# Forming the first output tile of the first projection during its norm, and moving four modulation pieces to the pooling stage

## The reference, cut to what matters

```
mod_k = silu(c) @ mod_w[k] + mod_b[k]        # k = 0, 1, 2; for c and c_ctx; 1024 x 3072 weights each
h     = layer_norm(x) * (1 + scale) + shift  # shift, scale: the first two thirds of mod_0
p     = h @ w_in                             # 2304 rows x 1024, by 1024 x 4224: 33 tiles of 128 output columns
pool  = (windowed means of p[:, :256] - p[:, :256]) @ pool_w * pool_scale
```

## Time and profile before

| what | us |
|---|---|
| median of 3 runs | 6125.97 (6121.39 to 6126.76) |
| profiled execution, its own time | 6124.45 |
| its span | 6122.5 |
| norm block | about 61 to 251 |
| projection block | about 251 to 1099 |
| pooling block | about 1099 to 1161 |

### The profile page before, as it was taken

One profiled execution on the slowest core, in us unless ns is written; L12 is line 12 of the kernel. 1 busy time (PEld: TensorE's weight loads), 2 busy tenths in 40 slices (PEclk: granted clock), 3 DMA queues, 4 the chain that ended last, 5 costly groups with the idle time before them and its releaser, 6 DMA issues. The chain is left out here.

```text
span 6122.5 us, 127440 instructions
## 1 busy us (share of the span) xinstructions
PE 5220.1 (85%) x55385; PEld 3996.1 (65%) x55385; DVE 3363.5 (55%) x5004; ACT 1889.2 (31%) x2998; POOL 1754.5 (29%) x1381
## 2 busy tenths in 40 slices
PE   6799999599997566587999659999897999688989
PEld 1488888488886455476888435555476888445667
DVE  2226656444444666476895268888755000307877
ACT  1224444233333443134111214444413000015652
POOL 2201111245443555035000006666635111000012
PEclk8899999799998888798999779999998999888999
DMA  6424434211121110373322320000074211221035
GB/s 201 139 97 154 153 139 156 84 60 61 55 64 69 41 52 29 131 230 123 109 105 81 125 87 22 17 16 20 30 220 136 71 67 71 78 69 75 31 108 160
DMA packets 430043, 572.37 MB, mean 93 GB/s; under 512 B 66470, under 2 KB 318246, under 8 KB 416766
## 3 DMA queue, kind: packets, MB, share of 16 engines
q1 hardware_dynamic: 364886, 391.37, 20.3%
q10 hardware_dynamic: 49272, 115.65, 4.9%
q0 software_dynamic: 15344, 57.45, 2.4%
HBM read 361.26 MB, written 203.12 MB: 92 GB/s over the span
## 5 line engine op out<-in xcount | busy, mean ns | idle before, releaser
L157 PE MATMUL p_bank<-p_hT_high,p_w_high 128*128 128x512 f32 (+1 forms) x2784 | 1053.7, 378 | 20.9 <-DVE p_w_low L151 17.0
L158 PE MATMUL p_bank<-p_hT_low,p_w_high 128*128 128x512 f32 (+1 forms) x2784 | 1045.4, 376 | 0.0
L159 PE MATMUL p_bank<-p_hT_high,p_w_low 128*128 128x512 f32 (+1 forms) x2784 | 1045.2, 375 | 0.0
L157 PEld LDWEIGHTS p_bank<-p_hT_high,p_w_high 128*128 128x128 f32 x2784 | 525.4, 189 | 123.9 <-DVE p_w_low L151 17.3
L159 PEld LDWEIGHTS p_bank<-p_hT_high,p_w_low 128*128 128x128 f32 x2784 | 525.7, 189 | 95.5
L158 PEld LDWEIGHTS p_bank<-p_hT_low,p_w_high 128*128 128x128 f32 x2784 | 525.8, 189 | 93.3
L2796 POOL TENSOR_TENSOR at_acc<-at_acc,at_p 128x512 f32<-128x512 f32 x256 | 423.6, 1655 | 143.7 <-ACT at_p L2734 122.5
L2734 ACT ACTIVATE at_p<-at_sc 128x1024 f32<-128x1024 f32 (+1 forms) x296 | 284.8, 1012 | 401.1 <-PE at_sc L2625 349.2
L1519 PE MATMUL rsc_db<-rsc_W,rsc_TK 64*64 64x64 f32 x8640 | 384.4, 219 | 6.8 <-issue 6.5
L2838 DVE TENSOR_REDUCE at_mx<-at_mb 128x2 f32<-128x1024 f32 (+1 forms) x280 | 342.1, 1222 | 79.7 <-PE at_mb L2636 77.6
L157 PE MATMUL o_bank<-o_w_high,o_m_high 128*128 128x512 f32 x800 | 314.7, 393 | 61.9 <-POOL o_m_low L151 61.9
(11 more groups left out here) (396 smaller groups left out, 10661.9 us busy)
## 6 DMA issues: line engine op xcount, KB each, us to landing
rsc_X<-rwkv_chunks SPq DMA_DIRECT2D x108, 320.0 KB, 4.6
pT<-p_o ACTq DMA_DIRECT2D x132, 256.0 KB, 2.4
rwkv_chunks<-p_arr POOLq DMA_DIRECT2D x54, 512.0 KB, 5.3
o_z<-pT SPq DMA_DIRECT2D x50, 512.0 KB, 5.3
o_y<-y SPq DMA_DIRECT2D x50, 512.0 KB, 6.7
pT<-p_eo ACTq DMA_DIRECT2D x96, 256.0 KB, 2.0
p_w<-in_w_in_dram SPq DMA_DIRECT2D x33, 512.0 KB, 4.2
x<-o_o ACTq DMA_DIRECT2D x32, 512.0 KB
```

The source lines that it names most:

```text
L157: nc.tensor.matmul(out, lhs[0], rhs[0], start=start, stop=False)
L158: nc.tensor.matmul(out, lhs[0], rhs[1], start=False, stop=False)
L159: return nc.tensor.matmul(out, lhs[1], rhs[0], start=False, stop=stop)
```

## The change

One output tile (the first of the projection) is multiplied inside the norm block, in quarters of 2 of its 8 contraction steps: from t = 5 on, PE runs one quarter at the end of each iteration, and the remaining 7 of 20 after the loop. Its weights are loaded behind x tile 0 and split by POOL ahead of tile 0's own split, through the buffer `hf[0]`. The next tile's weights are loaded into a part of `mw[0]` at t = 13 and split by ACT and DVE after the loop, before the block ends. The projection starts with tile 1. The norm block keeps 12 of the 16 pieces; the last four are done in the pooling block. The separate bias buffers `mb` are gone: the bias is loaded into `mo`, the buffer in which the sum is formed and from which it is stored, and the wait ahead of that load is now for the store of piece t-2.

```diff
@@ project_rwkv
-    w_part = [[...] for u in range(2)]
+    w_part = [[...], first_part]
-            for n in range(M):
-                if n >= 1:
-                    sp.wait_ge(w_split, n)
+            for n in range(2, M):
+                if n >= 3:
+                    sp.wait_ge(w_split, n - 2)
...
-            for n in range(M):                       # PE
+            for n in range(1, M):
...
-            cast_weights(0)
-            cast_weights(1)
+            cast_weights(2)
@@ norm_project
-    PIECES = [(l, c * MC) for l in range(len(later)) for c in range(3 * D // MC)]
+    PIECES = [(l, c * MC) for l in range(len(later)) for c in range(3 * D // MC)][:12]
...
-        EARLY = 0 if later else 2
+        EARLY = 1 if later else 2
...
                         if q >= 2:
-                            sp.wait_ge(mo_full, q - 1)
-                        sp.dma_start(mb[q % 2][:], later[l][3][c:c + MC].partition_broadcast(2)).then_inc(mw_full[q % 2], 16)
+                            sp.wait_ge(mo_out[q % 2], q // 2 * 16)
+                        sp.dma_start(mo[q % 2][:], later[l][3][c:c + MC].partition_broadcast(2)).then_inc(mw_full[q % 2], 16)
...
+                        if later and t == len(PIECES) + 1:
+                            sp.wait_ge(mw_free, len(PIECES))
+                            sp.dma_start(w_next, wv[:, :, NEXT * P:(NEXT + 1) * P]).then_inc(w_full[1], 16)
...
+                        elif later and t == 0:        # ACT, before it writes hf[0]
+                            act.wait_ge(w_split, 1)
...
+                    if later:                         # ACT, after the loop
+                        early_store((N - LAG - 4) // 4)
+                        for c in range((N - LAG - 4 + 3) // 4, PER_TILE):
+                            early_out(c)
+                            if c == PER_TILE - 1:
+                                act.wait_ge(w_full[1], 16)
+                                nc.scalar.copy(w_part[0][0][:], w_next).then_inc(w_high, 1)
+                            early_store(c)
+                        act.wait_ge(e_out[0], 16 * PER_TILE)
...
                     def biased(q):
                         dve.wait_ge(mw_free, q + 1)
-                        if q >= 2:
-                            dve.wait_ge(mo_out[q % 2], q // 2 * 16)
-                        nc.vector.tensor_tensor(mo[q % 2][:], mp[q % 2][0:2, 0:MC], mb[q % 2][:], ALU.add).then_inc(mo_full, 1)
+                        dve.wait_ge(mw_full[q % 2], (q // 2 + 1) * 32)
+                        nc.vector.tensor_tensor(mo[q % 2][:], mp[q % 2][0:2, 0:MC], mo[q % 2][:], ALU.add).then_inc(mo_full, 1)
@@ pool_branch
+                for q, c in enumerate(PIECES):        # SP, after u and the constants; 4 pieces
+                    sp.dma_start(mo[q][:], mod_b[c:c + MC].partition_broadcast(2)).then_inc(mw_full[q], 16)
+                    sp.dma_start(mw[q][:], mod_w.rearrange("(p k) n -> p k n", k=KT)[:, :, c:c + MC]).then_inc(mw_full[q], 16)
...
                 for t in range(2):                    # PE
+                    if t:
+                        for q in range(2):
+                            piece(q)
                     pe.wait_ge(pooled_ready, t + 1)
...
+                for q in range(2, 4):
+                    piece(q)
```

More of the change, by code:

```diff
@@ L194, in project_rwkv @@
     w_sb = s.sb("w0", [P, KT, P])
-    w_part = [[s.sb(f"w{u}_{part}", [P, KT, P], F32R) for part in ("high", "low")] for u in range(2)]
+    w_part = [[s.sb(f"w1_{part}", [P, KT, P], F32R) for part in ("high", "low")], first_part]
     w_full, w_high, w_split = s.sem("w_full"), s.sem("w_high"), s.sem("w_split")
@@ L531, in _ @@
             dve.wait_ge(prm_ready, 1)
-            for n in range(2, LEAD):
+            for n in range(3, LEAD):
                 split(n)
@@ L568, in weight_tiles @@
             return tiles, parts, s.sems("w_full", 2), s.sem("w_high"), s.sem("w_split")
-        EARLY = 0 if later else 2
-        if EARLY:
+        EARLY = 1 if later else 2
+        if later:
+            COLS = [(rwkv[0] + 9, True)]
+            NEXT = rwkv[0] + 10
+            w_part = [[s.sb(f"w0_{part}", [P, KT, P], F32R) for part in ("high", "low")]]
+            w_full, w_high, w_split = s.sems("w0_full", 2), s.sem("w0_high"), s.sem("w0_split")
+            NO = 1
+        else:
             weights = weight_tiles()
@@ L574, in norm_project @@
             NO = 3
[L575 removed]
+        if EARLY:
+            eo, e_out = [] if later else [s.sb(f"eo{u}", [P, NT]) for u in range(NO)], s.sems("e_out", NO)
             UNITS = [(c, e) for c in range(len(CHUNKS)) for e in range(EARLY) if c < 4 or COLS[e][1]]
             PER_TILE = len(UNITS) // EARLY
[L578 removed]
+            SHARES = 4 // EARLY
+            HALVES = [(u, h) for u in range(len(UNITS)) for h in range(SHARES)]
             LAG = 5
@@ L603, in norm_project @@
                 mw = [s1.sb(f"mw{u}", [P, KT, MC]) for u in range(2)]
-                mb = [s1.sb(f"mb{u}", [2, MC]) for u in range(2)]
                 mo = [s1.sb(f"mo{u}", [2, MC]) for u in range(2)]
-                mp = s1.banks(2)
+                w_next = mw[0][:, :, 0:P]
+                mp = [ctx1.enter_context(nc.psum_tensor(f"{name}n_mod{u}", [P, NT], F32)) for u in range(2)]
                 cond_in, act_ready = s1.sem("cond_in"), s1.sem("act_ready")
@@ L656, in _ @@
                             load_x(t + NX)
-                        if EARLY and t in (4, 6):
+                        if later and t == len(PIECES) + 1:
+                            sp.wait_ge(mw_free, len(PIECES))
+                            sp.dma_start(w_next, wv[:, :, NEXT * P:(NEXT + 1) * P]).then_inc(w_full[1], 16)
+                        if not later and t in (4, 6):
                             n = EARLY + (t - 4) // 2
@@ L875, in _ @@
                             half(t - 1)
-                        if EARLY and t >= LAG + 4 and (t - LAG - 4) % 4 == 0:
+                        if not later and t >= LAG + 4 and (t - LAG - 4) % 4 == 0:
                             early_out((t - LAG - 4) // 4)
@@ L881, in _ @@
                         half(N - 1)
-                    if EARLY:
+                    if later:
+                        dve.wait_ge(w_high, 2)
+                        split_low(nc.vector, w_part[0][1][:], w_next, w_part[0][0][:]).then_inc(w_split, 1)
+                    else:
                         for c in range((N - LAG - 4 + 3) // 4, PER_TILE):
@@ L1299, in pool_branch @@
         ps = s.banks(4)
+        MC = 384
+        PIECES = [c * MC for c in range(4, 3 * D // MC)]
+        mod_c, mod_c_ctx, mod_w, mod_b, mod_out = later
+        cond, cond_act = s.sb("cond", [P, 2, KT]), s.sb("cond_act", [P, KT, 2])
+        mw = [s.sb(f"mw{q}", [P, KT, MC]) for q in range(4)]
+        mo = [s.sb(f"mo{q}", [2, MC]) for q in range(4)]
+        mp = [ctx.enter_context(nc.psum_tensor(f"pool_mod{q}", [P, NT], F32)) for q in range(4)]
+        cond_in, act_ready, mw_full = s.sem("cond_in"), s.sem("act_ready"), s.sems("mw_full", 4)
+        mod_sum, mod_bias, mod_stored = s.sem("mod_sum"), s.sem("mod_bias"), s.sem("mod_stored")
         zeroed, const_in, u_in = s.sem("zeroed"), s.sem("const_in"), s.sem("u_in")
@@ L1340, in _, with piece @@
                                             ).then_inc(pooled_ready, 1)
+                for q in range(len(PIECES)):
+                    dve.wait_ge(mod_sum, q + 1)
+                    dve.wait_ge(mw_full[q], 32)
+                    nc.vector.tensor_tensor(mo[q][:], mp[q][0:2, 0:MC], mo[q][:], ALU.add).then_inc(mod_bias, 1)
             @block.tensor
             def _(pe):
+                def piece(q):
+                    pe.wait_ge(mw_full[q], 32)
+                    for k in range(KT):
+                        mm = nc.tensor.matmul(mp[q][0:2, 0:MC], cond_act[:, k, :], mw[q][:, k, :], start=(k == 0), stop=(k == KT - 1))
+                    mm.then_inc(mod_sum, 1)
+                pe.wait_ge(act_ready, 1)
                 for t in range(2):
+                    if t:
+                        for q in range(2):
+                            piece(q)
                     pe.wait_ge(pooled_ready, t + 1)
```

59 lines of the change are left out of this document (37 added, 22 removed).

## The result

Slower, by about what was forecast. The changed kernel takes 6151.39 us (median of six runs, 6146.68 to 6159.86); the kernel before, measured beside it, 6127.93 (6121.39 to 6130.17). The ratio is 1.004, with a 95% interval of 1.0029 to 1.0052: +23.5 us where +26.8 was forecast. One execution of the kernel before (8879.64 us) and one of experiment 6 (13864.68) ran with a granted clock of 0.56 to 0.57 over the whole and are left out of all medians here.

A forecast was written before the change was run, and what follows sets the result against it. The norm block was taken as bound by a ring of waits, the projection by PE, and pooling's PE as waiting for DVE. Projection end +19.9 and pooling +6.9 made +26.8 us on 6124.45, forecast median 6153, range 6134 to 6190.

The forecast's parts named there:

- The turn: Norm loop, t = 2 to 11: stats of neighbouring tiles come 16.5 us apart, against 10.1 before.
- The two choices: Low ends taken within the turn: store landing 1.6 us (mostly 5.5 before), x landing 3.3 (range 3.1 to 7.8).
- this ring: Norm loop: the x load waits behind the bias load for the previous store's landing, closing once per tile, 16.5 us.
- Tile 13's stats: Norm loop: they come at 253.8 us, against 187.37 before, including 1.3 for the early tile's load.
- The last four tiles: Norm loop from t = 12, no piece loads: 6.1 us per tile, tile 17's stats at 278.2, 16.7 back.
- The tail: Norm block's end, tile 17's stats to tile 1's first matmul: 23.9 us, bounds 20 and 28.
- the comparison of like with like: Projection: without tile 0, first tile still paying 27.64 us, its end comes 19.9 us later.
- Pooling: Pooling block with four moved pieces: next stage starts 6.9 us later, bounds +3 and +11.
- A: Rival, norm loop: the wait hides behind the other x buffer, turns stay 10.1 us, 6088 us; chance 0.08.
- B: Rival, norm loop: each store lands in 5.5 us, ten turns add 39 us, 6192 us; chance 0.11.
- C: Rival, about the same: loop clock stays up, landings least, tail and pooling at lower bounds, 6135 us; chance 0.11.
- could cost up to 1.7 each: Early quarters on PE: free in 16.5 us turns, but up to 1.7 us each with turns of 10.1.

The follow-up runs named there:

- experiment 6: Kernel before plus only the early output tile and next tile's weight split, bias in own rows, all 16 pieces in the norm block: 6089.93 us, ratio 0.9940.
- experiment 2: Kernel before with only the bias loaded into `mo` behind the store of piece t-2: 6219.75 us, ratio 1.0148.
- experiment 1: Changed kernel with the bias in rows of its own and its load waiting for DVE's addition again, not the store: 6092.94 us, ratio 0.9935.
- 9: Kernel before with six unread matmuls added on PE to each norm-loop iteration from t = 5: 6119.24 us, ratio 0.9980.
- experiment 5: Kernel before with only the last four modulation pieces moved to the pooling block: 6112.78 us, ratio 0.9980.
- 3: Changed kernel, store wait kept, but SP issues the x load ahead of the bias load and its wait: 6101.33 us, ratio 0.9955.
- 4: Changed kernel with POOL issuing the store of piece t-2 ahead of tile t's split: 6126.51 us, ratio 0.9996.
- 7: Changed kernel with own bias rows and old wait; in pooling one piece ahead of the first matmul set, three between the sets: 6084.58 us, ratio 0.9930.
- 8: Kernel 7 with the x load issued ahead of the bias load and its short wait: 6088.89 us, ratio 0.9937.

## Why the prediction was right

**The turn.** Its terms against the turn from 155.15 to 171.98:

| term | forecast | measured |
|---|---|---|
| stats to `xn` done | 2.74 | 2.75 |
| `xn` to ACT | 2.07 | 2.07 |
| ACT to POOL | 3.07 | 3.06 |
| POOL to the store's issue | 3.45 | 3.45 |
| the store's landing | 1.6 | 1.60 |
| bias issue to x issue | 0.30 | 0.30 |
| x landing, to DVE's start | 3.3 | 3.60 |
| sum | 16.5 | 16.83 |

This is the longest of the nine; their mean is 16.65. The two choices held. Taking the store's low end was right for the reason given: in this ring the 1.5 MB loads are over by then (DMA share 0.01). The x landing, 3.4 to 3.6, was put 0.1 to 0.3 low. PE's idle time, "some 5 us", is 7.0; the transposes take 1.97 all the same. The Trainium skill, "DMA: Bandwidth & Descriptors", in its section on one DMA issued by GpSimd, has a fixed part of about 2.0 us; here these stores release their waiter 1.6 to 1.7 us after the issue, and the measurement decides.

**Tile 13's stats** came at 255.0, 1.2 after the forecast.

**The last four tiles** took 27.4 us, not 24.4. Here the forecast treated a tile as 6.1 whatever POOL does. One `xn` of these stands beside POOL's subtraction (276.23 to 278.57):

```profile
276.22 2.89 DVE L857 TENSOR_SCALAR p1n_xn<-p1n_x,p1n_ag,p1n_sd 128x1024 f32<-128x1024 f32 x1
```

The same instruction takes 0.81 alone. That is 2.1 of the 3.0. The traces of all eleven kernels hold 198 such passes up to 330 us. The 114 with no POOL subtraction beside them take 0.81 to 0.83; the longest, 2.9 to 3.1, each stand beside a whole one. No run took the subtraction away, so the cause is suggested by the times and not tested. The kernel before has it too (2.99 at 189.30).

**The tail** took 23.0 us from tile 17's stats, not 23.9. With the three misses before it (1.2 and 3.0 late, 0.9 back), tile 1's first matmul was 3.3 late, and the projection's end +21.8 instead of +19.9: the projection itself was 1.4 shorter than by the comparison of like with like. The term is the first tile: the forecast let tile 1 pay tile 0's 27.64, and it took 26.26 (305.40 to 331.66).

**Pooling** added 4.9, not 6.9. The term that was too large is the end: from the last matmul at 1184.98 to the scan's load at 1187.72 is 2.7 us, where bias 0.5 and 3.98 had been put down. It lies within the bounds that were given (+3 to +11). The close hit is partly luck: 1.2 and 3.0 late, and 0.9, 1.4 and 2.0 early cancel to +26.7 at the scan's load against +26.8.

**The median** moved 23.5. The 3.2 below what the trace has at the scan are inside what the runs scatter.

**The rivals.** A (the wait hides, 6088) fell by the turns of 16.65 and by experiment 2, where the wait alone costs 90.7 us. Its number is close to experiment 1's 6092.94, since it priced the same kernel: the change with no turn of more than 10.1. B (stores of 5.5) fell by the landings of 1.6 to 1.7. C asked for a clock that stays up; it was 0.79 in the loop, transposes 1.97. The range was said to go from C to B, but its top, 6190, is 2 below B's 6192.

**What was wrong** is a remark that the sum did not use: in a loop with turns of 10.1 the quarters "could cost up to 1.7 each". Experiments 6 and 9 show the opposite sign. With a quarter, or six unread matmuls, in PE's idle time the last eight turns fall from 10.2 to 9.5 and 9.1. A step that adds work to a part-idle PE has to be priced by the clock too, not by its own length alone.

**Where the whole change stands.** The wait costs 58 us by the medians (change against experiment 1), the rest gains 36. Most of this gain is the early tile: it alone gives 35 (experiment 6); the moved pieces alone give 12.5 (experiment 5), after paying 5 us in pooling as they are placed. The medians do not add up, the traces nearly do: at the scan's first load 30.8 and 7.5 make 38.3, and both together (experiment 1) 36.6. Against the kernel before, in us, the trace up to that load and the median say:

| kernel | scan's first load | median |
|---|---|---|
| changed | +26.7 | +23.5 |
| 1 | -36.6 | -36.1 |
| 2 | +92.2 | +90.7 |
| 3 | -29.4 | -27.7 |
| 4 | -3.9 | -2.5 |
| 5 | -7.5 | -12.5 |
| 6 | -30.8 | -35.3 |
| 7 | -41.0 | -40.7 |
| 8 | -38.6 | -36.4 |
| 9 | -9.1 | -12.6 |

No two figures of a row are more than 5 us apart, and one trace's stages behind the scan's first load differ from another's by up to 13. So the change's stages explain the medians of all ten kernels, and differences of a few us between two kernels are not to be read from medians.

## What to carry to other kernels

When a buffer is made to serve both a load and a store, the load's wait becomes the store's landing; price it by the whole way round, the landing and everything that stands before the store's issue on its engine, times the iterations. Then look at what stands behind that wait in its queue: here a 3 KB load that nobody needed soon held a 512 KB load that everybody needed, and either two rows of memory (58 us) or another order of two issues (50 us) undid it. Such an order matters while the wait is the longest way round; with the short wait it gave nothing.

## What the runs showed of the hardware

- Matmuls of 1.66 us whose result is not read, put into PE's idle time in each iteration, raised the granted clock of that stretch from 0.83 to 1.00 and shortened the kernel by 0.2% (ratio 0.9980, 0.9971 to 0.9989).
- A DVE pass over 128x1024 took 2.89 us beside a POOL subtraction and 0.81 alone; of 198 such passes in eleven traces, none with no subtraction beside it took over 0.83.
- The stores out of `mo` take 1.6 to 1.7 us in a quiet ring (DMA share 0.01), where the earlier trace rows had a median of 5.5, and experiment 1, with the weights issued ahead again, 5.4: the same transfer, other company.
